# A transformer feed-forward with seven block products in place of eight, its weight sums on GpSimd

## The reference

```
hf = rms_norm(x, norm_ffn) @ w_up          # 2048 -> 8192
return x + jnp.square(jax.nn.relu(hf)) @ w_down   # 8192 -> 2048
```

## Time and profile before

| | |
|---|---|
| median of 3 runs | 3805.63 us (3805.61 to 3812.92) |
| profiled execution, first to last instruction | 3805.8 us |
| TensorE busy | 3571.4 us, 94% |
| VectorE, ScalarE, GpSimd busy | 46%, 34%, 18% |
| feed-forward stage | about 2224 to 3788 us |
| output stage | about 3788 to 3806 us |

### The profile page before, as it was taken

The page is one execution under the profiler, slowest core; times in us unless marked ns, Lnnn a source line. Parts: engine busy times, 40 slices in busy tenths (PEclk is TensorE's granted clock), DMA queues, the critical chain, the costliest instruction groups (busy, mean ns, idle before and its releaser), DMA issues. The chain is left out here.

```text
span 3805.8 us, 65517 instructions
## 1 busy us (share of the span) xinstructions
PE 3571.4 (94%) x26210; PEld 3317.2 (87%) x26210; DVE 1762.8 (46%) x2737; ACT 1299.2 (34%) x1953; POOL 679.0 (18%) x431
## 2 busy tenths in 40 slices
PE   7999998875897999999988999999999999999998
PEld 7999997554746888888868999999999999999998
DVE  4222223764556777777774343333333333333333
ACT  3111111332125777777773231222221222221222
POOL 0000000000004888888850000000000000000000
PEclk9999999767978999999998999999999999999999
DMA  7433442106637999999975322222222222222221
GB/s 209 113 109 105 112 113 88 52 22 211 152 127 260 332 333 331 336 331 331 332 274 159 88 78 89 88 83 86 89 89 89 89 84 83 89 89 89 89 86 62
DMA packets 458084, 568.51 MB, mean 149 GB/s; under 512 B 41250, under 2 KB 331984, under 8 KB 457812
## 3 DMA queue, kind: packets, MB, share of 16 engines
q1 hardware_dynamic: 457812, 564.64, 46.1%
HBM read 518.08 MB, written 46.49 MB: 148 GB/s over the span
## 5 line engine op out<-in xcount | busy, mean ns | idle before, releaser
L71 PE MATMUL f_acc<-xf_hi,ffn_hi 128*128 128x272 f32 x2048 | 594.4, 290 | 0.0
L69 PE MATMUL f_acc<-hidden_hi,ffn_lo 128*128 128x272 f32 x2048 | 591.6, 289 | 2.8 <-DVE mix_t L2467 2.8
L71 PE MATMUL f_acc<-hidden_hi,ffn_hi 128*128 128x272 f32 x2048 | 592.8, 289 | 0.0
L69 PE MATMUL f_acc<-xf_hi,ffn_lo 128*128 128x272 f32 x2048 | 591.4, 289 | 0.5
L70 PE MATMUL f_acc<-hidden_lo,ffn_hi 128*128 128x272 f32 x2048 | 590.7, 288 | 0.0
L70 PE MATMUL f_acc<-xf_lo,ffn_hi 128*128 128x272 f32 x2048 | 588.7, 287 | 0.0
L1695 POOL TENSOR_TENSOR dc_vl<-dc_vpages,dc_vh 128x1024 fp32r<-128x1024 f32 x241 | 573.6, 2395 | 12.0 <-ACT dc_vh L2034 11.7
L2418 ACT ACTIVATE ffn_hi<-ffn_raw 128x2048 fp32r<-128x2048 f32 x127 | 242.3, 1908 | 619.3 <-PE f_acc L71 619.3
L69 PE MATMUL z_acc<-xn_hi,win_lo 128*128 128x280 f32 (+1 forms) x1536 | 446.2, 290 | 1.1 <-DVE win_lo L303 1.1
L71 PE MATMUL z_acc<-xn_hi,win_hi 128*128 128x280 f32 (+1 forms) x1536 | 446.7, 291 | 0.0
L70 PE MATMUL z_acc<-xn_lo,win_hi 128*128 128x280 f32 (+1 forms) x1536 | 445.5, 290 | 0.0
(11 more groups left out here) (375 smaller groups left out, 6197.3 us busy)
## 6 DMA issues: line engine op xcount, KB each, us to landing
dc_kpages<-in_cache_k SPq DMA_DIRECT2D x256, 512.0 KB, 5.4
dc_vpages<-in_cache_v SPq DMA_DIRECT2D x256, 512.0 KB, 5.2
ffn_raw<-in_w_up SPq DMA_DIRECT2D x64, 1024.0 KB, 6.3
ffn_raw<-in_w_down SPq DMA_DIRECT2D x64, 1024.0 KB, 5.0
win_raw<-in_w_in SPq DMA_DIRECT2D x48, 1024.0 KB, 6.3
ffn_raw<-in_w_out SPq DMA_DIRECT2D x16, 1024.0 KB, 6.2
z_scratch<-z_out SPq DMA_DIRECT2D x48, 280.0 KB, 2.1
sm_c<-in_state_C SPq DMA_DIRECT2D x32, 256.0 KB, 6.6
```

What stands on the lines that cost most here:

```text
L69: nc.tensor.matmul(out, wlo, xhi, start=first, stop=False)
L71: return nc.tensor.matmul(out, whi, xhi, start=False, stop=last)
```

## The change

The two products of the feed-forward are made by a scheme that multiplies 2x2 block matrices with seven block products in place of eight, at the price of sums of blocks. The blocks are halves of the depth, pairs of 128 output features, and the halves of the tokens. The work is 64 units: unit 0 the plain way, units 1 to 31 the rest of `w_up`, units 32 to 63 `w_down` in four blocks of the hidden depth. A unit has seven steps of 8 slices by three passes (24 matmuls), each with its own weight operand (one of the four blocks, or one of four sums `sum1` to `sum4`, made by GpSimd in place in the loaded weights and in `ff_s1`) and its own activation operand (seven, kept split in `xh` and `xl`). ScalarE makes the high part of a weight operand (`high`), VectorE the low part (`low`), in three buffers. Partial sums in PSUM are held by ScalarE (`hold`) and joined by VectorE (`join`); in the up half ScalarE applies relu and square and GpSimd makes the four differences that the second product needs (`combine`); all seven parts are stored to HBM (`hq_dram`) and read back as operands (`operand`, `op_high`, `op_low`) before units 32, 40, 48 and 56. In the down half GpSimd adds the results to running sums that come from and go to HBM (`add_top`). At the start the normalized activations are made first (a reciprocal and 16 normalizing instructions), then four sums of them by GpSimd. The last eight units turn and store their results themselves; `emit` is gone. `finish_and_project` no longer splits a first tile for the feed-forward, and stores its rows to HBM.

```diff
-def exact_passes(nc, out, whi, wlo, xhi, xlo, first, last):
-
-    nc.tensor.matmul(out, wlo, xhi, start=first, stop=False)
-    nc.tensor.matmul(out, whi, xlo, start=False, stop=False)
-    return nc.tensor.matmul(out, whi, xhi, start=False, stop=last)
+def exact_passes(nc, out, whi, wlo, xhi, xlo, first, last, resumed=False):
+
+    nc.tensor.matmul(out, wlo, xhi, start=first, stop=False, skip_group_check=resumed)
+    nc.tensor.matmul(out, whi, xlo, start=False, stop=False, skip_group_check=resumed)
+    return nc.tensor.matmul(out, whi, xhi, start=False, stop=last, skip_group_check=resumed)
...
+            def keep(n):
+                sp.wait_ge(added, n + 1)
+                sp.dma_start(acc_dram[n * P:(n + 1) * P, :], xt[:, n, :]).then_inc(feed.kept, 16)
+
+            for n in range(N - GROUP):
+                sp.wait_ge(flow.lo_made, n + 1)
+                sp.dma_start(tile(flow.raw, n % GROUP), w[:, :, (n + GROUP) * P:(n + GROUP + 1) * P])\
+                    .then_inc(flow.landed[n % GROUP], 16)
+                if n >= 2:
+                    keep(n - 2)
+            for v in range(2):
+                sp.dma_start(feed.raw[:, v, :].rearrange("p (k n) -> p k n", n=2 * P), up[v][:, :, 0:2 * P])\
+                    .then_inc(feed.landed[v], 16)
+            for n in range(N - GROUP - 2, N):
+                keep(n)
...
-            act.wait_ge(ffn.landed[0], 16)
-            act.wait_ge(flow.used, N - 1)
-            nc.scalar.activation(ffn.hi[:, 0, :], ffn.raw[:, 0, :], ACT.Copy).then_inc(ffn.hi_made, 1)
...
-def mlp(nc, d, a, sems, xhi, xlo, xt, flow, sumsq):
...
+STEPS = 7
+HQ = (0, 1, 4, 3, 5, 2, 6)
...
+def feed_forward(nc, d, a, sems, c, mix, feed, sumsq, acc_dram, hq_dram, y_prompt, y_sample):
...
+    H, KH, PAIRS = d.ohalf, d.kc // 2, d.ff // (2 * P)
+    OUTS = d.kc // 2
+    UNITS, LAST = 2 * PAIRS, 2 * PAIRS - OUTS
+    FIRST = 4
+    assert PAIRS == 4 * OUTS and KH == 8 and 2 * H == d.to
+    step = lambda u, i: i if u == 0 else FIRST + STEPS * (u - 1) + i
...
+        xh, xl = (sb(f"ff_x{n}", [P, STEPS, KH, H], F32R) for n in ("hi", "lo"))
+        whi, wlo = (sb(f"ff_w{n}", [P, 3, KH, P], F32R) for n in ("hi", "lo"))
+        total = sb("ff_s1", [P, KH, P])
+        held = sb("ff_held", [P, 3, H])
...
+        source = lambda u, i: (kv(u, 0)[:, 0], kv(u, 1)[:, 0], kv(u, 0)[:, 1], kv(u, 1)[:, 1])[i] if u == 0 else \
+            (kv(u, 0)[:, 0], kv(u, 1)[:, 0], kv(u, 0)[:, 0], total[:, :, :], kv(u, 0)[:, 1], kv(u, 1)[:, 0],
+             kv(u, 1)[:, 1])[i]
+        last_of_block = lambda u: u >= PAIRS - 1 and u % OUTS == OUTS - 1 and u < UNITS - 1
+        first_of_block = lambda u: u >= PAIRS and u % OUTS == 0
+        block_of = lambda u: (u - PAIRS) // OUTS
...
+            def more(u, v):
+                if u >= 1 and u + 2 < UNITS:
+                    sp.wait_ge(lo_made, step(u, 4 if v == 0 else 6) + 1)
+                    if v == 0:
+                        sp.wait_ge(summed, 4 * u)
+                    weights(u + 2, v)
+
+            def keep_hidden(u):
+                sp.wait_ge(combined, 4 * u + 4)
+                x, b = piece(u), u // OUTS
+                sp.dma_start(hq[b][:, 0, u % OUTS, :], x[:, 0, :]).then_inc(h_stored[u % 2], 16)
+                sp.dma_start(hq[b][:, 1:7, u % OUTS, :], x[:, 2:8, :]).then_inc(h_stored[u % 2], 16)
...
+            def operand(u, i):
+                sp.wait_ge(used, step(u, i) + 1)
+                b = block_of(u + 1)
+                if i == 0:
+                    for r in range(2):
+                        sp.wait_ge(h_stored[r], 32 * (OUTS // 2) * (b + 1))
+                sp.dma_start(xl[:, i, :, :].bitcast(F32).rearrange("p k t -> p (k t)"), hqx[b][HQ[i]]).then_inc(op_in[i], 16)
...
+            for u in range(1, UNITS):
+                turn = last_of_block(u)
+                if u == PAIRS:
+                    keep_hidden(u - 1)
+                if u >= PAIRS:
+                    load_top(u)
+                if PAIRS < u <= LAST:
+                    keep_top(u - 1)
+                if turn:
+                    operand(u, 0)
+                    operand(u, 1)
+                if u < PAIRS and not turn:
+                    more(u, 0)
+                    keep_hidden(u - 1)
+                    more(u, 1)
+                elif turn:
+                    more(u, 0)
+                    operand(u, 2)
+                    if u < PAIRS:
+                        keep_hidden(u - 1)
+                    operand(u, 3)
+                    more(u, 1)
+                    for i in range(4, STEPS):
+                        operand(u, i)
+                else:
+                    more(u, 0)
+                    more(u, 1)
+                if u > LAST:
+                    send(u - 1)
...
+            T = nc.gpsimd.tensor_tensor
+
+            def sum1(u):
+                for v in range(2):
+                    pool.wait_ge(landed[base(u) + v], 16 * nth(u))
+                if u >= 2:
+                    pool.wait_ge(lo_made, step(u - 1, 3) + 1)
+                T(total[:, :, :], kv(u, 0)[:, 1], kv(u, 1)[:, 1], ALU.add).then_inc(summed, 1)
+
+            def sum3(u):
+                pool.wait_ge(summed, 4 * (u - 1) + 1)
+                T(kv(u, 0)[:, 1], kv(u, 0)[:, 0], kv(u, 0)[:, 1], ALU.subtract).then_inc(summed, 1)
+
+            def sum2(u):
+                pool.wait_ge(summed, 4 * (u - 1) + 2)
+                pool.wait_ge(lo_made, step(u, 0) + 1)
+                T(kv(u, 0)[:, 0], total[:, :, :], kv(u, 0)[:, 0], ALU.subtract).then_inc(summed, 1)
+
+            def sum4(u):
+                pool.wait_ge(summed, 4 * (u - 1) + 3)
+                pool.wait_ge(lo_made, step(u, 1) + 1)
+                T(kv(u, 1)[:, 0], kv(u, 1)[:, 0], kv(u, 0)[:, 0], ALU.subtract).then_inc(summed, 1)
+
+            nc.gpsimd.memset(over[:, :], 1.0 / d.dm).then_inc(over_made, 1)
+            pool.wait_ge(x_hi, d.kc)
+            pool.wait_ge(x_lo, d.kc)
+            T(xn(1, 1), xn(1, 1), xn(0, 1), ALU.subtract).then_inc(t_made, 1)
+            pool.wait_ge(t_made, 1)
+            T(xn(0, 1), xn(0, 1), xn(0, 0), ALU.subtract).then_inc(t_made, 1)
+            pool.wait_ge(t_made, 2)
+            T(xn(0, 0), xn(0, 0), xn(1, 1), ALU.add).then_inc(t_made, 1)
+            pool.wait_ge(t_made, 3)
+            T(xn(1, 0), xn(1, 0), xn(0, 0), ALU.subtract).then_inc(t_made, 1)
+
+            def combine(u):
+                z = piece(u)
+                pool.wait_ge(squared, u + 1)
+                T(z[:, 4, :], z[:, 1, :], z[:, 0, :], ALU.subtract).then_inc(combined, 1)
+                T(z[:, 6, :], z[:, 3, :], z[:, 1, :], ALU.subtract).then_inc(combined, 1)
+                pool.wait_ge(combined, 4 * u + 2)
+                T(z[:, 5, :], z[:, 3, :], z[:, 4, :], ALU.subtract).then_inc(combined, 1)
+                pool.wait_ge(combined, 4 * u + 3)
+                T(z[:, 7, :], z[:, 2, :], z[:, 5, :], ALU.subtract).then_inc(combined, 1)
+
+            def add_top(u):
+                pool.wait_ge(acc_in[u % 2], 16 * ((u - PAIRS) // 2 + 1))
+                for done in (c11, c12, c22, copied21):
+                    pool.wait_ge(done, u)
+                T(tops(u), tops(u), piece(u).rearrange("p m t -> p (m t)"), ALU.add).then_inc(added, 1)
+
+            sum1(1)
+            sum3(1)
+            for u in range(1, UNITS):
+                sum2(u)
+                sum4(u)
+                if u - 1 < PAIRS:
+                    combine(u - 1)
+                elif u - 1 < LAST:
+                    add_top(u - 1)
+                if u + 1 < UNITS:
+                    sum1(u + 1)
+                    sum3(u + 1)
...
+            def high(u, i):
+                g = step(u, i)
+                if g >= 3:
+                    act.wait_ge(used, g - 2)
+                if u == 0:
+                    if i < 2:
+                        act.wait_ge(landed[i], 16)
+                elif i in (0, 1):
+                    act.wait_ge(landed[base(u) + i], 16 * nth(u))
+                elif i < 6:
+                    act.wait_ge(summed, 4 * (u - 1) + (3, 1, 2, 4)[i - 2])
+                A(whi[:, g % 3, :, :], source(u, i)).then_inc(hi_made, 1)
+
+            def hold(u, s, b, i, done):
+                act.wait_ge(used, step(u, i) + 1)
+                if u >= 2:
+                    act.wait_ge((c11, c12, c22)[s], u - 1)
+                A(held[:, s, :], acc[u % 2][b][:, 0:H]).then_inc(done, 1)
...
+            def relu_square(u):
+                for done in (c11, c12, c22):
+                    act.wait_ge(done, u)
+                act.wait_ge(copied21, u)
+                z = piece(u)[:, 0:4, :]
+                A(z, z, ACT.Relu).then_inc(relued, 1)
+                act.wait_ge(relued, u + 1)
+                A(z, z, ACT.Square).then_inc(squared, 1)
...
+            def op_high(u, i):
+                act.wait_ge(op_in[i], 16 * (block_of(u + 1) + 1))
+                A(xh[:, i, :, :], xl[:, i, :, :].bitcast(F32)).then_inc(op_hi, 1)
+
```

(78 more changed lines are left out.)

463 lines of the change are left out of this document (233 added, 230 removed).

## The result

The changed kernel's median is 3713.94 us (3712.25 to 3719.5, 4 runs), beside 3807.05 (3805.61 to 3812.92, 4 runs) for the kernel before: ratio 0.975, 95% interval 0.9736 to 0.9764. The profiled execution spans 3717.8 us; it is the slowest of the four runs (3719.5). The forecast was 3717.

A forecast was written before the change was run, and what follows sets the result against it. TensorE's matmul streaming was taken to bound the feed-forward; 191.3 + 8 - 37 - 56 - 8 - 9 = 89 us gained on a span of 3805.8 gave 3717 us, range 3665 to 3840.

The forecast's parts named there:

- The bound and what is removed: Feed-forward lasts as long as its matmuls stream; 1,512 fewer at 126.5 ns gain 191.3 us, a unit takes 21.25 us.
- Do the engines exclude each other: Weight-split subtractions on VectorE exclude GpSimd's instructions, joins don't; shared demand is 95 to 99% of a unit.
- The walk of the prediction: Dated order of GpSimd and VectorE instructions in one up unit: every deadline met, the tightest by 0.9 us.
- Steady units' imperfect order, 9 us: Allowance in the steady feed-forward units for imperfect order: 0.15 us a unit, 9 us over 62.
- the row of 3.75 us: Profile row before: a 64x4 VectorE instruction kept out over two GpSimd subtractions, read as a sign GpSimd can hold on.
- The start: First feed-forward units: unit 2 starts about 90 us into the stage, costing 37 us more than before; bounds 20 and 55.
- The four turns: Before units 32, 40, 48 and 56, operand reads, copies and splits cost 14 us each, 56 in all; bounds 6 and 25 each.
- Small terms: Ten transposes in TensorE's queue in each of the last units cost 8 us; stored sums in the projection stage cost nothing.
- Tail: After the last matmul: one add, ten transposes, copies and the last store, 11.5 us, 8 less than before.
- GpSimd holds on: Rival: VectorE is kept out between GpSimd instructions in the feed-forward, 167 us, 3884; chance 0.24 with anything longer than 3798.
- Saturated: Rival: engines alternate but GpSimd instructions cost some tenths more, units average 21.9 us, +40 us, 3757, up to 3798; chance 0.18.
- Exclusion costs little: Rival: start 6 us, turns 24 and the 9 us less, 3678; chance 0.13 for below 3690.

The follow-up runs named there:

- the seventh run: Changed kernel with three more GpSimd subtractions of 272 columns in every unit, each waiting for the one before: 3783.35 us.
- the fourth run: Changed kernel with one unused VectorE instruction of 4 columns ahead of the split of step 2 in down units 35 to 55: 3714.57 us.
- The third run: Changed kernel with the four activation sums at the start made by VectorE instead of GpSimd, weight sums still on GpSimd: 3708.07 us.

## Why the prediction was right, point by point

**The bound and what is removed.** Held. 62 units at 21.185 us against 21.25 counted for matmuls alone: 4 us less.

**Do the engines exclude each other.** Held, and it was the open question of the case. The timelines of one steady up unit, GpSimd then VectorE:

```profile
2603.84 0.78 POOL L2596 TENSOR_TENSOR mix_t<-mix_t 128x272 f32<-128x272 f32 x1
2604.70 1.64 POOL L2598 TENSOR_TENSOR mix_t<-mix_t 128x272 f32<-128x272 f32 x1
2606.41 0.78 POOL L2600 TENSOR_TENSOR mix_t<-mix_t 128x272 f32<-128x272 f32 x1
2607.14 3.44 POOL L2565 TENSOR_TENSOR ff_s<-mix_t 128x1024 f32<-128x1024 f32 x1
2610.66 3.27 POOL L2569 TENSOR_TENSOR mix_t<-mix_t 128x1024 f32<-128x1024 f32 x1
...
2618.77 2.40 POOL L2579 TENSOR_TENSOR mix_t<-mix_t 128x1024 f32<-128x1024 f32 x1 [1.23 <-DVE ff_wlo L2746]
```
```profile
2604.01 1.69 DVE L2746 TENSOR_TENSOR ff_wlo<-ffn_raw,ff_whi 128x1024 fp32r<-128x1024 f32 x1 [1.83 <-ACT ff_whi L2623]
...
2606.68 1.59 DVE L2746 TENSOR_TENSOR ff_wlo<-ffn_raw,ff_whi 128x1024 fp32r<-128x1024 f32 x1 [0.63 <-ACT ff_whi L2623]
2609.71 1.96 DVE L2746 TENSOR_TENSOR ff_wlo<-ffn_raw,ff_whi 128x1024 fp32r<-128x1024 f32 x1 [1.44 <-ACT ff_whi L2623]
...
2618.90 3.35 DVE L2746 TENSOR_TENSOR ff_wlo<-mix_t,ff_whi 128x1024 fp32r<-128x1024 f32 x1
```

Take the VectorE row at 2606.68. GpSimd's difference had begun at 2606.41 and ended at 2607.19; the split ended 1.08 us after that, at 2608.27, and sum 1, which GpSimd began at 2607.14 without any wait, ended at 2610.58, 2.31 us after the split. The splits at 2604.01 and 2609.71 went in the same way, 1.08 and 1.09 us behind the end of the GpSimd instruction they met (2604.62, 2610.58). So did the split at 2618.90, which waited for sum 4 (to 2621.17) and ended 1.08 us after it. The walk of the prediction has these instructions in this order but for one: the fourth difference (2606.41) ran ahead of the split of step 5, not behind it. The other dates hold within 0.7 us. Its tightest one, step 2, is the one that the seventh run found, with 1.2 us of slack where the walk had 0.9. One condition of the walk was too strict: it let VectorE in only where GpSimd waits for its own last result, but sum 1 had no such wait, and the split got in ahead of its work.

The rule of the Trainium skill, "SBUF — State Buffer", section "SBUF: two separate sides", that the shared pair is held for a whole instruction by whichever starts first, is borne out by these rows and by the fourth run (an instruction of four columns took 2.30 us), with the joins' 0.43 us as its other side.

**Steady units' imperfect order, 9 us.** Zero. The walk needed no such term; it came from the row of 3.75 us, which recurs in the decode stage but in no unit of the feed-forward. With the 4 us above this is the largest error, 13 us too many.

**The start.** 90.3 predicted, 111.8 - 21.2 = 90.6 measured from the stage's own beginning. The parts held too. GpSimd's last activation sum, its first weight sum, and the matmul that ends the hole:

```profile
2280.66 5.70 POOL L2590 TENSOR_TENSOR mix_t<-mix_t 128x2176 f32<-128x2176 f32 x1
2286.30 4.53 POOL L2565 TENSOR_TENSOR ff_s<-ffn_raw 128x1024 f32<-128x1024 f32 x1
...
2301.62 0.56 PE L69 MATMUL ff_acc<-ff_xhi,ff_wlo 128*128 128x272 f32 x1 [16.62 <-DVE ff_xlo L2763]
```

The first sums ended 56.1 us into the stage (56.6 predicted), TensorE resumed at 71.3 (72.4) after 16.6 us idle (17.7). The granted clock was 0.50 in the hole, the 1.2 GHz level. The third run confirms the mechanism: without the shared port and the slower engine in that chain 9.4 us go.

**The four turns.** 56 predicted, 64.6 measured. Both causes that were named act: an operand lands 12.6 us after its issue and its copy stood before the holds in the scalar engine's queue, and VectorE had no room. The page's row of the transfers, and the critical chain through the change behind unit 39 (start, length):

```profile
ff_xlo<-hq_scratch SPq DMA_DIRECT2D x28, 1088.0 KB, 12.6
```

```profile
3131.47 15.04 DMA ff_xlo<-hq_scratch
3146.56 1.91 issue
3148.47 1.05 ACT ff_whi L2623
...
3150.68 0.43 DVE mix_t L2753
3151.11 4.48 DVE ff_xlo L2768
3155.60 3.44 DVE ff_wlo L2746
```

The mis-sized term is the first, the scalar engine's. I priced a scalar engine 6 to 8 us late, 24 to 32 us over four turns, and the first halves, which hold that delay, came to 36.6. The other 6 to 8 us of my 14 a turn went to VectorE without a working of their own, and the second halves, 28.0 us in sum, agree with them (13.5 once GpSimd no longer holds the port for weight sums, 3.2 without seven eighths of the operand splits). Two rows of ScalarE, the fifth operand's copy and the hold that step 2 needs, show it at unit 39, which began at 3122.2:

```profile
3154.84 2.02 ACT L2623 ACTIVATE ff_xhi<-ff_xlo 128x2176 fp32r<-128x2176 f32 x1 [2.20 <-DMA ff_xlo<-hq_scratch]
...
3157.71 0.38 ACT L2623 ACTIVATE ff_held<-ff_acc 128x272 f32<-128x272 f32 x1
```

The fifth operand landed 32.6 us behind the start of the unit, where I had 29 to 32, and the hold ended 8.6 us later than the 27.3 of the prediction. The split of step 2 ended later still, so that the step began 9.6 us late, because GpSimd lengthened two VectorE instructions ahead of it (4.48 and 3.44 us in the chain, where 2.41 and 1.21 are their times alone). I had counted the scalar engine alone for this delay.

**Small terms.** Seven units with transposes, 22.27 - 21.19 = 1.08 each: 7.5 against 8. Tail: 11.0 against 11.5. The stage began 5.8 us later than before, at 2230.27, a difference that arises ahead of it; over the runs here it began between 2222.2 and 2236.0.

**Sum.** 3716.8 - 13 + 8.6 + 0.3 - 1.0 + 5.8 = 3717.5, against 3717.8. That the forecast of the time is closer than its terms is luck: the 13 us too many and the 8.6 with the 5.8 too few cancel. The prediction also added nothing from span to time, where in the runs here the time is 1.7 to 2.1 us longer. Against the median of 3713.94 the forecast is 3 us too long; the medians differ by 93.1 us and the two profiled spans by 88.0, where 89 were forecast.

**The rivals.** "GpSimd holds on" is refuted for this stage by the steady units and by the fourth run, though the decode stage has seven such rows. "Saturated": the seventh run shows its edge at 1.2 us more GpSimd work a unit, but the edge was not reached. "Exclusion costs little" took 6 us off the start and 24 off the turns; the start came out at 90.6 against 90.3, the turns 8.6 longer, so it was wrong on both and right on the 9 us.

## What to carry to other kernels

Where two engines lock each other out for whole instructions, add their demand on the lock and walk the dates of one period in order: at 95 to 99% the walk said that it fits, and it fitted, with 1.2 us to spare. But a fit in steady state is no gain: moving the sums to GpSimd bought nothing there, and cost 17.5 us at the turns and, with the activation sums, 11.5 at the start (111.8 against 100.3), where the locked-out engine was the one that TensorE waited for. And where each of two limits can hide the other, take them away together before pricing either: one alone gave 10.8 or 24.2 us, both 58.1.

## What was not expected of the hardware

- An instruction of VectorE of 128x4 elements that starts 0.12 us behind a GpSimd subtraction takes 2.30 us, and it gets in between two GpSimd instructions that have no wait between them. In the decode stage an instruction of 64x4 was kept out over two of them seven times of seven (3.75 to 3.77 us). The time for changing over is small: a split ended 1.08 us behind the GpSimd instruction in its way, where it takes 1.22 from the start.
- A GpSimd subtraction of 2,176 columns takes 4.9 us and one of 1,024 2.39; VectorE's take 2.43 and 1.22. Beside GpSimd's long ones, each 1.22 us of VectorE became 5.0 to 5.8.
- After gaps of equal length (3.7 to 3.8 us) in the same stretch of two runs the granted clock was 1.00 in one and 0.50 in the other.
- At the turns an operand of 1.1 MB landed in 12.6 us (median of 28), where single weight loads land in 6.6 to 7.1. Short transfers cut the first halves from 36.6 to 12.4 us, and moving the operand copies one place later cut them to 18.3 with transfers as long as before, so most of that loss was work that stood in the queue behind a waiting copy.
